# Loading x in quarters, turning it unscaled, and applying the token's factor where u, v, the gates, q and k leave PSUM

## The reference, cut to what matters

```
h = rms_norm(x, norm1_w)            # x * rsqrt(mean(x*x) + 1e-6) per token, times norm1_w per column
z = h @ w_in                        # 2048 x 8192: u, q, k, v, gate_s, gate_a
y_ssm  = s5_mixer(u, ...)           # a state-space scan over the tokens
y_attn = diff_attention(rms_norm(q heads), rms_norm(k heads), v, ...)
m = sigmoid(gate_s) * (y_ssm @ w_proj_ssm) + sigmoid(gate_a) * (y_attn @ w_proj_attn)
```

## Time and profile before

| what | value |
|---|---|
| time, median of 3 runs (lowest, highest) | 2423.23 us (2420.42, 2423.9) |
| profiled execution: its span, the only time shown for it | 2420.8 us |
| TensorE matmuls busy | 2346.3 us, 97% of the span |
| VectorE busy | 1465.8 us, 61% |
| ScalarE busy | 1129.3 us, 47% |
| chain that ended last | TensorE 82%, VectorE 12%, ScalarE 3%, issue 2%, transfers 1% |
| mean rate from and to memory | 172 GB/s |

### The profile page before, as it was taken

How to read it: one execution, slowest core, us unless ns; L and a number is a source line. 1 busy time by engine, 2 the same in 40 slices (tenths; PEclk the granted TensorE clock), 3 DMA queues, 4 the chain that set the end, 5 groups by cost and what they waited for, 6 DMA issues and landing times.

```text
span 2420.8 us, 38838 instructions
## 1 busy us (share of the span) xinstructions
PE 2346.3 (97%) x16401; PEld 2025.2 (84%) x16401; DVE 1465.8 (61%) x1852; ACT 1129.3 (47%) x1566; POOL 196.8 (8%) x200
## 2 busy tenths in 40 slices
PE   7999999999999999999999999999999999999997
PEld 7777777888888888888888899889898899899985
DVE  4899966766554554454444445745755568456556
ACT  5565556644544444444444434433554535334542
POOL 4000000002000000000000001220000051301000
PEclk9999999999999999999999999999999999999998
DMA  9544454455566666666555576434547574335465
GB/s 245 157 157 148 155 193 149 163 193 182 183 191 186 188 191 184 191 191 191 189 191 189 190 222 177 118 98 116 165 132 244 168 216 141 98 106 156 139 208 168
DMA packets 260366, 415.77 MB, mean 172 GB/s; under 512 B 53448, under 2 KB 74440, under 8 KB 259424
## 3 DMA queue, kind: packets, MB, share of 16 engines
q1 hardware_dynamic: 254496, 395.63, 53.1%
q0 software_dynamic: 5376, 17.56, 2.5%
q10 hardware_dynamic: 320, 0.08, 0.0%
HBM read 406.90 MB, written 7.87 MB: 171 GB/s over the span
## 4 chain that ended last, share of the span: by engine, by line
PE 82%; DVE 12%; ACT 3%; issue 2%; DMA 1%; ACTq 0%; SPq 0%; DVEq 0%
PE banks L585 80%; DVE wp_hl L1166 4%; ACT wp_hl L1861 2%; DVE u_z L1497 1%; DVE nsd L1560 1%; DVE u_z L1479 0%; PE banks L697 0%; ACT L1861 0%; DMA raw<-w_in 0%; DVE r_SA L1701 0%; PE banks L709 0%; PE banks L822 0%; DMA xt<-x 0%; DVE xt L1478 0%; DVE r_SA L1667 0%
## 5 line engine op out<-in xcount | busy, mean ns | idle before, releaser
L1166 DVE TENSOR_TENSOR wp_hl<-raw,wp_hl 128x1024 fp32r<-128x1024 f32 x740 | 915.4, 1243 | 862.8 <-ACT wp_hl L1861 861.9
L1861 ACT ACTIVATE wp_hl<-raw 128x1024 fp32r<-128x1024 f32 x740 | 783.1, 1060 | 1087.3 <-PE banks L585 1054.5
L585 PE MATMUL banks<-wp_hl,XX_hl 128*128 128x512 f32 x3840 | 899.7, 393 | 10.5 <-DVE wp_hl L1166 10.5
L585 PEld LDWEIGHTS banks<-wp_hl,XX_hl 128*128 128x128 f32 x3840 | 715.8, 188 | 174.7 <-DVE wp_hl L1166 16.9
L585 PE MATMUL banks<-XX_hl,wp_hl 128*128 128x256 f32 x4992 | 646.2, 287 | 9.7 <-DVE wp_hl L1166 7.5
L585 PEld LDWEIGHTS banks<-XX_hl,wp_hl 128*128 128x128 f32 x4992 | 611.3, 192 | 28.0 <-issue 14.1
L585 PE MATMUL banks<-wp_hl,FF_hl 128*128 128x512 f32 x1056 | 240.7, 389 | 0.0
L585 PEld LDWEIGHTS banks<-wp_hl,FF_hl 128*128 128x128 f32 x1056 | 197.9, 188 | 41.0
L585 PE MATMUL banks<-wp_hl,MM_hl 128*128 128x512 f32 x384 | 88.4, 390 | 0.0
L585 PE MATMUL banks<-wp_hl,MXa_hl 128*128 128x512 f32 x384 | 88.3, 389 | 0.0
L585 PEld LDWEIGHTS banks<-wp_hl,MXa_hl 128*128 128x128 f32 x384 | 72.1, 188 | 14.9
(11 more groups left out here) (439 smaller groups left out, 1771.2 us busy)
## 6 DMA issues: line engine op xcount, KB each, us to landing
raw<-w_in SPq DMA_DIRECT2D x304, 512.0 KB, 3.9
raw<-w_out SPq DMA_DIRECT2D x96, 512.0 KB, 4.4
raw<-w_ffn_gate SPq DMA_DIRECT2D x88, 512.0 KB, 3.5
raw<-w_ffn_up SPq DMA_DIRECT2D x88, 512.0 KB, 3.5
raw<-w_ffn_down SPq DMA_DIRECT2D x88, 512.0 KB, 3.5
raw<-w_proj_attn SPq DMA_DIRECT2D x16, 512.0 KB, 4.2
raw<-w_proj_ssm SPq DMA_DIRECT2D x16, 512.0 KB, 3.6
raw<-w_glu SPq DMA_DIRECT2D x8, 512.0 KB, 3.6
```

What stands on the lines that cost most here:

```text
L585: return e.matmul(o, lhsT, rhs, start=start, stop=stop, skip_group_check=True)
L1166: return tt(d, src, hi, SUB)
L1861: return e.activation(o, x, func, bias=bias, scale=scale)
```

## The change

x comes in eight loads of 128 tokens by 512 columns (rows of 2 KB), two for each quarter, with pieces 0 to 3 between the quarters. TensorE turns each group of x with plain transposes as soon as its quarter is there. The squares move into the loop on ScalarE, one block a round; the roots move to round g = 8, behind the splits of the rounds before. At g = 9 TensorE multiplies a matrix of ones by `dg`, which gives the factor of each token in all partitions; ScalarE copies it to `rsd`. The factor then multiplies u on VectorE (both halves, ScalarE's copy goes), v on both engines, and the gates in ScalarE's sigmoid. For q and k the sums of squares are multiplied by its square (t = 11), and the reciprocal root by the factor (t = 13). norm1_w is loaded ahead of the other constants on ScalarE's queue.

```diff
@@ -378,7 +378,7 @@
     w1 = A["w_in"][0]
-    cols("u", 2, w1, 0, 16, "AV")
+    cols("u", 2, w1, 0, 16, "VV")
     cols("q", 2, w1, 1024, 16, "AA", tokens=True)
@@ -524,10 +525,10 @@
     def _(e):
-        for h in range(2):
+        def quarter(c):
+            w = slice(512 * c, 512 * c + 512)
             for t in range(2):
-                c = slice(1024 * h, 1024 * h + 1024)
-                e.dma_start(xt[:, t, c], A["x"][0, 128 * t:128 * t + 128, c]).then_inc(s_x[h], 16)
+                e.dma_start(xt[:, t, w], A["x"][0, 128 * t:128 * t + 128, w]).then_inc(s_x[c], 16)
@@ -540,8 +541,14 @@
-        for p in range(4):
-            weights(p)
+        quarter(0)
+        weights(0)
+        weights(1)
+        quarter(1)
+        weights(2)
+        weights(3)
+        quarter(2)
+        quarter(3)
         e.dma_start(cst[:, 128:COLS_AT], A["consts"][:, 128:COLS_AT]).then_inc(s_s5, 16)
@@ -683,7 +690,7 @@
             if stage == 0:
-                e.wait_ge(*XD("d", stage))
+                e.wait_ge(s_x[g // 2], 32)
             elif stage < 3:
@@ -691,10 +698,7 @@
                     src, o = (xr if stage == 3 else xt)[:, t, 256 * g + 128 * k:256 * g + 128 * k + 128], 256 * k + 128 * t
-                    if stage == 0:
-                        last = mm(B[b][:, o:o + 128], src, dg[:, 128 * t:128 * t + 128], o == 0, o == 384)
-                    else:
-                        last = e.transpose(B[b][:, o:o + 128], src, ident)
+                    last = e.transpose(B[b][:, o:o + 128], src, ident)
             last.then_inc(XTR.made("t", n), 1)
@@ -726,6 +730,10 @@
                     turned_x(stage, g)
+                if stage == 0 and g == 9:
+                    bank(6, *XR("r"))
+                    e.wait_ge(*XD("d"))
+                    mm(B[6][:, 0:256], M["ones"], dg, True, True).then_inc(XRP.made("p"), 1)
                 if g > 1:
@@ -1175,16 +1183,17 @@
                 e.wait_ge(*over(j.name))
-            if n in HOME:
-                c, dst = int(l), HOME[n]
-                e.tensor_copy(pair(dst, 2 * c + 1), b[1]).then_inc(s_evV, 1)
+            if n == "u":
+                e.wait_ge(*XR("r"))
+                for i in range(2):
+                    tt(uT[:, 4 * int(l) + 2 * i:4 * int(l) + 2 * i + 2, :], v3(b[i], 2), wide3(rsd, 2, 256), MUL).then_inc(s_evV, 1)
             elif n in ("cq", "cc", "pq"):
...
                 c = int(l)
-                e.tensor_copy(vM[:, 1, 512 * c:512 * c + 512], b[1]).then_inc(s_evV, 1)
+                ts(vM[:, 1, 512 * c:512 * c + 512], b[1], rs[:, 3:4], None, MUL).then_inc(s_evV, 1)
             elif n in ("vn0", "vn1"):
@@ -1336,13 +1344,16 @@
         e.tensor_copy(pcol[:, 0:16], B[5][:, 0:16]).then_inc(PCV.made("c1"), 1)
-        roots(0)
         e.wait_ge(*PCV("c1"))
         for g in range(10):
-            if g < 3:
+            if 0 < g < 3:
                 split(g)
...
                 rest_of_x(0, g)
+            if g == 0:
+                split(0)
+            elif g == 8:
+                roots(0)
             if g > 1:
@@ -1487,9 +1498,19 @@
                 s_result(t - 1)
-            if t == 13:
+            of_half = lambda i: qkn.rearrange("p (z i x) -> p i z x", z=2, i=2)[:, i]
+            if t == 11:
+                e.wait_ge(*DA("q", 7))
+                for i in range(2):
+                    last = ts(of_half(i), of_half(i), rs[:, 2 + i:3 + i], rs[:, 2 + i:3 + i], MUL, MUL)
+                last.then_inc(DR.made("x"), 1)
+            elif t == 13:
                 e.wait_ge(*DQ("s"))
-                e.reciprocal(qkn, qkn).then_inc(DR.made("r"), 1)
+                e.reciprocal(qkn, qkn).then_inc(DR.made("c"), 1)
+                e.wait_ge(*DR("c"))
+                for i in range(2):
+                    last = ts(of_half(i), of_half(i), rs[:, 2 + i:3 + i], None, MUL)
+                last.then_inc(DR.made("r"), 1)
             e.wait_ge(*ROT("zi", t))
@@ -1904,11 +1925,9 @@
             b = [B[x] for x in j.banks]
-            if n not in ("pa", "ps", "wo", "fd", "rk", "rv", "rr", "ch", "cb") and n[:2] not in ("fu", "xo"):
+            if n not in ("u", "pa", "ps", "wo", "fd", "rk", "rv", "rr", "ch", "cb") and n[:2] not in ("fu", "xo"):
                 e.wait_ge(*over(j.name))
-            if n in HOME:
-                act(pair(HOME[n], 2 * int(l)), b[0], ACT.Copy).then_inc(s_evA, 1)
-            elif n in ("cq", "cc", "pq"):
+            if n in ("cq", "cc", "pq"):
                 act(pair({"cq": cq, "cc": cu, "pq": qp}[n], 0), b[0], ACT.Copy).then_inc(s_evA, 1)
@@ -1925,14 +1944,16 @@
                 c = int(l)
-                act(vM[:, 0, 512 * c:512 * c + 512], b[0], ACT.Copy).then_inc(s_evA, 1)
+                e.wait_ge(*XD("r"))
+                act(vM[:, 0, 512 * c:512 * c + 512], b[0], ACT.Identity, scale=rs[:, 2:3]).then_inc(s_evA, 1)
             elif n in ("vn0", "vn1"):
...
             elif n in ("gs", "ga"):
+                e.wait_ge(*XD("r"))
                 for i in range(2):
                     d = pair(sgs(int(l)), i) if n == "gs" else pair(sga, 2 * int(l) + i)
-                    act(d, b[i], ACT.Sigmoid).then_inc(s_evA, 1)
+                    act(d, b[i], ACT.Sigmoid, scale=rs[:, 2 + i:3 + i]).then_inc(s_evA, 1)
             elif n in ("rg", "mg0", "mg1"):
@@ -1999,26 +2020,29 @@
-        HOME = {"u": uT}
+        e.dma_start(first_row[0:16, :], A["norm1_w"][0].rearrange("(a b) -> a b", a=16)).then_inc(s_n1, 16)
         for a, b in ((0, 128), (COLS_AT, NFIRST)):
             e.dma_start(cst[:, a:b], A["consts"][:, a:b]).then_inc(s_ones, 16)
-        e.dma_start(first_row[0:16, :], A["norm1_w"][0].rearrange("(a b) -> a b", a=16)).then_inc(s_n1, 16)
         e.preload_act_table(ACT.Sqrt)
         at.limit("gs2")
-        for h in range(2):
-            for t in range(2):
-                e.wait_ge(s_x[h], 32)
-                for q in range(2):
-                    w = slice(1024 * h + 512 * q, 1024 * h + 512 * q + 512)
-                    squares(0, 4 * t + 2 * h + q, 4 * h + 2 * t + q, xt[:, t, w])
-        e.wait_ge(s_ones, 32)
-        roots(0)
         e.wait_ge(*PCV("c1"))
         for g in range(10):
-            if g < 3:
+            if 0 < g < 3:
                 split(g)
...
                 rounded_x(0, g)
+            if g == 0:
+                split(0)
+            if g < 8:
+                c, t = g // 2, g % 2
+                e.wait_ge(s_x[c], 32)
+                squares(0, 4 * t + c, g, xt[:, t, 512 * c:512 * c + 512])
+            elif g == 8:
+                e.wait_ge(s_ones, 32)
+                roots(0)
+            else:
+                e.wait_ge(*XRP("p"))
+                act(rsd, B[6][:, 0:256], ACT.Copy).then_inc(XR.made("r"), 1)
             if g > 1:
@@ -2084,7 +2108,7 @@
             if t == 12:
-                e.wait_ge(*DA("q", 7))
+                e.wait_ge(*DR("x"))
                 act(qkn, qkn, ACT.Sqrt, bias=K["eps6"], scale=1.0 / 64).then_inc(DQ.made("s"), 1)
...
         main(at.go(4))
```

More of the change, by code:

```diff
@@ L431, in program @@
     s_ones, s_cst, s_pos, s_n1, s_par = sem("s_ones"), sem("s_cst"), sem("s_pos"), sem("s_n1"), sem("s_par")
-    s_x = [sem("s_x0"), sem("s_x1")]
+    s_x = [sem(f"s_x{c}") for c in range(4)]
     s_back, s_s5, s_at, s_tp, s_sk, s_hb, s_lora, s_out = (sem("s_back"), sem("s_s5"), sem("s_at"), sem("s_tp"), sem("s_sk"), sem("s_hb"), sem("s_lora"),
@@ L453, in program @@
     XQ, XS, XA, XD = marks("x_sq", "q"), marks("x_sum", "s"), marks("x_root", "s"), marks("x_diag", "r", "d")
+    XRP, XR = marks("x_row_t", "p"), marks("x_row", "r")
     XTR, NH, NL, LY = marks("x_turn", "t"), marks("x_hi", "h"), marks("x_lo", "l"), marks("ln_y", "y")
@@ L467, in program @@
     DP, DA, DB, DN = marks("tbl", "t"), marks("dn_sq", "q"), marks("dn_t", "t"), marks("dn_v", "n")
-    DQ, DR, DC = marks("dn_root", "s"), marks("dn_rec", "r"), marks("dn_c", "c")
+    DQ, DR, DC = marks("dn_root", "s"), marks("dn_rec", "x", "c", "r"), marks("dn_c", "c")
     def qk_block(m):
```

## The result

| kernel | time, median of 20 runs (lowest, highest) | ratio to before, 95% interval | span of the profiled execution |
|---|---|---|---|
| before | 2421.74 us (2418.58, 2423.9) | | 2420.8 us |
| changed | 2427.34 us (2424.72, 2431.48) | 1.0024 [1.0018, 1.0030] | 2426.2 us |

A forecast was written before the change was run, and what follows sets the result against it. TensorE bounds the entry with little lead over the loads; VectorE sets the pace from 90 to 320 us. Terms 1.8 + 0.6 + 0.6 = +3.0 us on 2423.2 gave 2426.2 us, range 2422.5 to 2430.2 us.

The forecast's parts named there:

- the early start: TensorE's entry: piece 0 at 12.6 instead of 18.47 us, all lead then lost waiting for loads; gain counted as 0.
- the loads of x at nothing: SyncE's queue: four more loads, about 2.1 us of issue, hidden by a full queue; cost 0, later pieces land as before.
- rival (d): SyncE has no cover for the added issues: piece 8 lands 2.1 us later, sum +5.1 us, 2428.3; chance 0.06.
- The chain's term: Sum, root, reciprocal and diagonals behind piece 8's split; TensorE waits, piece 7 begins at 45.0 instead of 43.22 us: +1.8 us.
- Rival (a): TensorE's clock falls in a new gap, 6.9 us at half rate: +6.4 us in all, 2429.6; chance 0.17.
- the forecast of a steady clock: TensorE's granted clock shows no 0.5 before 76 us, despite gaps of 2.8 and 3.0 us; no cost.
- u1: Where u1 leaves PSUM: two VectorE multiplies replace a copy on each of two engines, +0.6 us (0.59 to 0.68).
- Norms: Norms of q and k: four small VectorE operations added where VectorE is always busy, +0.6 us.

The follow-up runs named there:

- The quarters alone: The kernel before with only x's loads changed: eight loads of 512 columns, all ahead of piece 0; 2423.04 us, ratio 1.0007.
- the halves: The changed kernel with x in four loads of 1024 columns again, between the same weight pieces; 2425.76 us, ratio 1.0017 to the kernel before.

## Why the prediction was right or wrong

**What bounds the kernel, and the early start.** Right: the lead of TensorE ran into the loads and none was left. Its waits were forecast at 2.8 us ahead of piece 6 and 3.0 us ahead of the product. They came as 6.86 us ahead of piece 4 and 2.53 us ahead of the product. My own figures held a wait ahead of piece 4 that I did not name: with piece 0 at 12.6 us and 2.96 + 0.44 = 3.4 us a round, TensorE is done with its work at 26.2 us and takes piece 4 at 29.4. It grew because TensorE was done a microsecond sooner, at 32.09 - 6.86 = 25.2 us, and piece 4 landed 2.7 us late. Piece 6 then followed piece 5 without a wait. "ScalarE idle for weights until about 26.2, 35.4 and 41.0 us" was wrong: 28.93, 36.79 and 42.37 us.

**The failing step: the loads of x at nothing.** I wrote that SyncE has cover, since it "waits on a full queue there". It has little. The eight issues alone delayed piece 4 by 1.6 us in the kernel before, and in the changed kernel piece 8 came 1.4 us late in the profiled execution, 1.9 us in the mean of three. This was rival (d), priced at 2.1 us and given 0.06. The chain's term became 46.33 - 43.22 = 3.1 us instead of 1.8; its other parts were right (sum behind the low half, 1.4 us from sum to product, 0.32 us for the product). That the halves did not cure it means that (d)'s reason, the issue time, is not all of it. Between 8 and 10 us the changed kernel's transfers moved 255 GB/s against 390 before, and the halves' 284. The quarters alone kept 390 there, so loads of that size do not lower the rate by themselves; what does was not tried.

The Trainium skill, "DMA: Bandwidth & Descriptors", section "Bandwidth", which asks for transfers of a megabyte or more, pointed the right way here, in part by luck: the run with halves, whose loads are as large as before, shows that size alone is not it, and in the run with the quarters alone the time of the issues accounts for the whole delay of piece 4. That section of the Trainium skill gives its figures, from which I estimated 2.4 us, for loads that GpSimd issues; these are SyncE's.

**The clock.** Rival (a), given 0.17, happened besides, at the place it named: behind the wait for the product, 2.53 us long, the clock was at 0.5 for 3.4 us, and 1.7 us were lost. I had taken 6.9 us from the fall at 76 us in the trace of before, twice too long for this one. (That trace has another, which I did not read: the clock is at 0.5 from 1902.3 to 1912.5 us, from within a wait of 4.35 us on.) My argument against it, the dst waits of 1.6 us without a fall, was no bound for a wait of 2.5 us. And the clock fell once more, where I had named no gap: from 30.0 us, in the wait ahead of piece 4. By the signs that I gave, 0.5 in the clock column before 76 us, the forecast of a steady clock was wrong twice.

The Trainium skill, "TensorE: Matmul & The Clock Gate", section "HAM oscillation — how this bites in real kernels", describes this pattern, and the traces agree: the clock fell in the changed kernel's wait for piece 4, which is one for a load, and behind the waits of 2.4 to 3.6 us for the product in four executions, and it did not fall where that wait was 0.86 or 1.00 us.

**u1.** Right: 0.6 us forecast. The pair takes 1.28 us instead of 0.68, and the lag grows from 4.86 to 5.45 us.

**Norms.** 0.6 forecast, 0.83 measured: the first pair takes 0.42 us of VectorE, and the second holds the scan 0.42 us longer behind the reciprocal. The four are even dearer than end to end by my row, 0.73 us: they last 0.23 to 0.30 us each where the row had 0.18, so the row was too cheap for them.

**The sum by these steps** is 3.1 + 1.7 + 0.6 + 0.8 = 6.2 us. The scan of turn 13 is 289.98 - 283.53 = 6.45 us late. About 1 us comes back later: the same split of weights stands at 1644.48 us before and 1650.20 after, 5.7 us apart, and the spans end 5.4 us apart. What gives it back was not tried.

**Luck.** The sum is nearer to rival (a)'s 6.4 us than to the 3.0 us that were forecast, since two rivals, given 0.17 and 0.06, came true together. The time lay in the range because the range reached to (a). And 2427.34 looks closer to the forecast 2426.2 than the change was to 3.0 us, because the kernel before measured 2421.74 us in this series and not the 2423.23 us that I added to.

## What to carry to other kernels

An early start of the busiest engine is worth only as much as the loads behind it can follow: change start and load order together, since here either alone gave nothing or a loss (1.0000 and 1.0024) and both gave 0.9983. When a short chain moves into a dense stream, put the instruction that waits for it behind work that is ready; moving one product behind one piece let piece 8 begin 3.6 us sooner. Cost each added issue at full price on the queue, unless a row shows the queue standing idle.

## What was not expected of the hardware

- Four more issues of x went through to the next weights whole: 3.71 - 2.11 = 1.6 us of SyncE, and piece 4 landed 1.64 us later.
- Four loads in another order, with no more issues, in a kernel whose engines also start earlier, did nearly the same: pieces 4 and 8 landed 1.9 and 1.1 us later than in the profile of before.
- A wait of 2.39 us on TensorE was enough for the clock to fall, and the length of the fall differed: 3.4 us here, 6.8 us behind the 6.86 us wait for piece 4, 6.9 us behind the 3.73 us wait of the kernel before.
- Landings scatter more with the changed kernel's loads: piece 8 between 41.75 and 44.69 us in five executions, against 40.58 to 40.97 us in three of the kernel before.
